# Gate sums moved from GpSimd to VectorE, and a layer's small loads issued one by one along its projection

## What is computed

```python
h = rms_norm(x, norm1_g[l])
parts = jnp.split(h @ w_in[l], cuts, axis=-1)        # w_in: 1024 x 2144, q/k/v of four token mixers
o_a, o_b, o_c, o_d = four attention mixers, 256 wide each
...
br = jnp.stack([o_a, o_b, o_c, o_d], axis=2)
y = jnp.einsum('bsnc,ncd->bsnd', br, w_branch[l])    # four branches, 256 -> 1024
g = jax.nn.sigmoid(h @ w_gate[l] + b_gate[l]).reshape(B, S, N_BRANCH, D)
x = x + jnp.sum(g * y, axis=2) @ w_o[l]              # the gated sum over branches
h2 = rms_norm(x, norm2_g[l])
x = x + jnp.square(jax.nn.relu(h2 @ w_ff1[l])) @ w_ff2[l]
```

## Time and profile before

| | us |
|---|---|
| median of 3 runs (lowest to highest) | 840.53 (839.75 to 841.16) |
| the profiled execution, its own time | 840.49 |
| its span in the trace | 838.7 |
| TensorE products busy | 818.3 (98%) |
| VectorE busy | 540.9 (64%) |
| ScalarE busy | 411.1 (49%) |
| GpSimd busy | 83.6 (10%) |

### The profile page before, as it was taken

One profiled execution on the slowest core, in us unless ns is written; L12 is line 12 of the kernel. 1 busy time (PEld: TensorE's weight loads), 2 busy tenths in 40 slices (PEclk: granted clock), 3 DMA queues, 4 the chain that ended last, 5 costly groups with the idle time before them and its releaser, 6 DMA issues.

```text
span 838.7 us, 14823 instructions
## 1 busy us (share of the span) xinstructions
PE 818.3 (98%) x5763; PEld 750.5 (89%) x5763; DVE 540.9 (64%) x781; ACT 411.1 (49%) x698; POOL 83.6 (10%) x105
## 2 busy tenths in 40 slices
PE   7699999999999999999999999999999999999996
PEld 7699988999889999999999999799997999999995
DVE  6486566957667555666568756578756675555663
ACT  6346565655365333444464466466444553334442
POOL 3220000202310000000033000002221100000000
PEclk9899999999999999999999999999999999999999
DMA  8956633454437555555576755344344565565541
GB/s 254 246 167 209 172 108 101 121 182 150 127 100 229 199 200 196 184 167 184 178 194 201 220 151 153 127 123 128 109 167 129 192 218 190 200 200 190 171 141 50
DMA packets 100850, 141.09 MB, mean 168 GB/s; under 512 B 4796, under 2 KB 87040, under 8 KB 100800
## 3 DMA queue, kind: packets, MB, share of 16 engines
q1 hardware_dynamic: 99296, 137.12, 51.5%
q0 software_dynamic: 1216, 3.17, 1.5%
q10 hardware_dynamic: 288, 0.11, 0.1%
HBM read 139.33 MB, written 1.05 MB: 167 GB/s over the span
## 4 chain that ended last, share of the span: by engine, by line
PE 78%; issue 12%; DVE 4%; POOL 3%; DMA 2%; ACT 1%; POOLq 0%; ACTq 0%; DVEq 0%
PE bank_w L1185 16%; PE bank_w L1187 16%; PE bank_w L1186 16%; PE bank_acc L1185 8%; PE bank_acc L1186 8%; PE bank_acc L1187 8%; POOL mix L543 2%; DMA raw<-in_w_in 2%; DVE w_lo L808 2%; PE bank_acc L1281 2%; PE bank_acc L1293 1%; PE bank_o L1310 1%; DVE act_lo L1003 1%; DVE tmp L1023 1%; DMA cst<-in_table 0%
## 5 line engine op out<-in xcount | busy, mean ns | idle before, releaser
L808 DVE TENSOR_TENSOR w_lo<-raw,w_hi 128x1024 fp32r<-128x1024 f32 (+1 forms) x256 | 309.9, 1257 | 58.4 <-ACT w_hi L573 58.2
L1185 PE MATMUL bank_w<-act_hi,w_hi 128*128 128x256 f32 x1008 | 287.9, 286 | 0.0
L1187 PE MATMUL bank_w<-act_hi,w_lo 128*128 128x256 f32 x1008 | 285.8, 284 | 0.0
L1186 PE MATMUL bank_w<-act_lo,w_hi 128*128 128x256 f32 x1008 | 285.3, 283 | 0.0
L573 ACT ACTIVATE w_hi<-raw 128x1024 fp32r<-128x1024 f32 (+1 forms) x256 | 257.4, 1060 | 37.6 <-DMA raw<-in_w_in 19.8
L1185 PEld LDWEIGHTS bank_w<-act_hi,w_hi 128*128 128x128 f32 x1008 | 191.6, 190 | 7.1 <-ACT big L694 3.1
L1186 PEld LDWEIGHTS bank_w<-act_lo,w_hi 128*128 128x128 f32 x1008 | 190.9, 189 | 1.8 <-issue 0.5
L1187 PEld LDWEIGHTS bank_w<-act_hi,w_lo 128*128 128x128 f32 x1008 | 191.2, 190 | 0.0
L702 ACT ACTIVATE part_hi<-big 128x512 fp32r<-128x512 f32 x32 | 20.2, 633 | 189.8 <-DVE big L1038 187.1
L1185 PE MATMUL bank_acc<-w_hi,part_hi 128*128 128x512 f32 x256 | 100.3, 392 | 0.0
L1186 PE MATMUL bank_acc<-w_lo,part_hi 128*128 128x512 f32 x256 | 100.3, 392 | 0.0
(11 more groups left out here) (180 smaller groups left out, 983.6 us busy)
## 6 DMA issues: line engine op xcount, KB each, us to landing
raw<-in_w_ff SPq DMA_DIRECT2D x128, 512.0 KB, 4.9
raw<-in_w_gate SPq DMA_DIRECT2D x64, 512.0 KB, 4.7
raw<-in_w_in SPq DMA_DIRECT2D x32, 536.0 KB, 5.3
raw<-in_w_o SPq DMA_DIRECT2D x16, 512.0 KB, 4.8
raw<-in_w_branch SPq DMA_DIRECT2D x16, 256.0 KB, 4.6
raw<-in_w_branch SPq DMA_DIRECT2D x8, 512.0 KB, 4.2
xs<-in_x SPq DMA_DIRECT2D x2, 512.0 KB, 4.1
out_y<-big SPq DMA_DIRECT2D x4, 256.0 KB, 2.1
```

The lines of the kernel that those rows point to most:

```text
L808: nc.vector.tensor_tensor(half_view(w_lo, c, hf), raw_half(c, hf), f32(half_view(w_hi, c, hf)), ALU.subtract).then_inc(w_lo_ready, 1)
L1185: nc.tensor.matmul(dst, s_hi, m_hi, start=first, stop=False)
L1186: nc.tensor.matmul(dst, s_hi, m_lo, start=False, stop=False)
L1187: ins = nc.tensor.matmul(dst, s_lo, m_hi, start=False, stop=last)
```

## The change

GpSimd's 12 adds a layer (L543) are gone. VectorE makes each of them itself right behind its product (after a wait for that product's own semaphore), and no longer waits for `mixed` before it writes `tmp`. The last branch (`y` 3) is taken out of the step loop: its four quarters are written out with the `w_lo` halves of `o` 2 and the four `mix_lo` in between. The small loads of a layer are issued in groups, each of which waits until ScalarE has rounded the second half of a given chunk of the projection: the table `cst` (first layer only), both gains and the sink behind chunk 3; one half of the bias rows behind chunk 4; the other half behind chunk 5 and behind the inverse roots for mixer A; `w_uq` behind 6; `w_ukv` behind 7. `hi_count(l, c, h)` is the count of `w_hi_ready` at which half h of chunk c is rounded.

```diff
             for l in range(DEPTH):
                 norm(2 * l, l)
+                pool.wait_ge(w_hi_ready, hi_count(l, 3, 1))
                 if l == 0:
-                    pool.wait_ge(w_hi_ready, 5)
                     pool.dma_start(cst[:, C_ID + P:], table[:, C_ID + P:]).then_inc(cst_landed, 16)
-                for r in range(2):
-                    (bias row r: the same DMA as bias_run(l, r))
                 pool.dma_start(gain_qk[:, 0, :], ...)
                 pool.dma_start(gain_qk[:, 1, :], ...)
                 pool.dma_start(sink[:, :], ...)
-                pool.dma_start(w_uq[:, 0, :], ...)
-                pool.dma_start(w_uq[0:QR - P, 1, :], ...)
-                pool.dma_start(w_ukv[:, :], ...)
-                pool.wait_ge(sink_landed, l * 16 + 16)
-                nc.gpsimd.tensor_tensor(nsink[:, :], sink[:, :], neg_one[:, :], ALU.mult).then_inc(nsink_ready, 1)
+                pool.wait_ge(w_hi_ready, hi_count(l, 4, 1))
+                bias_run(l, 0)
                 pool.wait_ge(ss_a_ready, l + 1)
                 inverse_root(rs_a, ss_a, inv_head, l).then_inc(rs_a_ready, 1)
+                pool.wait_ge(w_hi_ready, hi_count(l, 5, 1))
+                bias_run(l, 1)
+                pool.wait_ge(sink_landed, l * 16 + 16)
+                nc.gpsimd.tensor_tensor(nsink[:, :], sink[:, :], neg_one[:, :], ALU.mult).then_inc(nsink_ready, 1)
+                pool.wait_ge(w_hi_ready, hi_count(l, 6, 1))
+                pool.dma_start(w_uq[:, 0, :], ...)
+                pool.dma_start(w_uq[0:QR - P, 1, :], ...)
+                pool.wait_ge(w_hi_ready, hi_count(l, 7, 1))
+                pool.dma_start(w_ukv[:, :], ...)
...
-                for k in range(4 * (NB - 1)):
-                    pool.wait_ge(y_read, l * 16 + (k + 5))
-                    if k >= 4:
-                        pool.wait_ge(mixed, l * 12 + (k - 3))
-                    nc.gpsimd.tensor_tensor(mix[:, k % 4, :], mix[:, k % 4, :], tmp[:, k % 2, :], ALU.add).then_inc(mixed, 1)
-                pool.wait_ge(mixed, l * 12 + 12)
                 norm(2 * l + 1, l)
...
                     k = 4 * (n - 1) + q
-                    if k >= 2:
-                        dve.wait_ge(mixed, l * 12 + (k - 1))
                     nc.vector.scalar_tensor_tensor(out=tmp[:, k % 2, :], in0=g, scalar=1.0, in1=y, op0=ALU.add,
                                                    op1=ALU.mult).then_inc(y_read, 1)
-                    if n == NB - 1 and 0 < q < 3:
-                        mix_lo(q - 1, l)
+                    dve.wait_ge(y_read, l * 16 + (k + 5))
+                    nc.vector.tensor_tensor(mix[:, q, :], mix[:, q, :], tmp[:, k % 2, :], ALU.add).then_inc(mixed, 1)
...
+                branch(NB - 1, l, (0,))
                 split_lo_half(POS["o", 2], 0, l)
+                branch(NB - 1, l, (1,))
+                mix_lo(0, l)
+                split_lo_half(POS["o", 2], 1, l)
+                branch(NB - 1, l, (2,))
+                mix_lo(1, l)
+                branch(NB - 1, l, (3,))
                 mix_lo(2, l)
-                split_lo_half(POS["o", 2], 1, l)
                 mix_lo(3, l)
                 split_lo(POS["o", 3], l)
```

More of the change, by code:

```diff
@@ L498, in norm, with bias_run @@
                     nc.gpsimd.tensor_tensor(rstd[:, t:t + 1], total, neg_half[:, 0:1], ALU.pow).then_inc(rstd_ready, 1)
+            def bias_run(l, r):
+                at = (NA_ROWS - 4 + r) * BIAS_ROW + NA_COLS - GRID_W
+                tables = b_rel_bias[bass.ds(l, 1), 0]
+                src = bass.AP(tensor=tables.tensor, offset=tables.offset + at,
+                              ap=[[1, GRID_W], [(2 * NA_ROWS - 1) * BIAS_ROW, H], [1, RUN]])
+                pool.dma_start(run[r * GRID_W:(r + 1) * GRID_W, :, :], src).then_inc(bias_landed, 16)
             for l in range(DEPTH):
                 norm(2 * l, l)
+                uq = d_w_uq[bass.ds(l, 1)].rearrange("o k n -> (o k) n")
+                pool.wait_ge(w_hi_ready, hi_count(l, 3, 1))
                 if l == 0:
-                    pool.wait_ge(w_hi_ready, 5)
                     pool.dma_start(cst[:, C_ID + P:], table[:, C_ID + P:]).then_inc(cst_landed, 16)
-                for r in range(2):
-                    at = (NA_ROWS - 4 + r) * BIAS_ROW + NA_COLS - GRID_W
-                    tables = b_rel_bias[bass.ds(l, 1), 0]
-                    src = bass.AP(tensor=tables.tensor, offset=tables.offset + at,
-                                  ap=[[1, GRID_W], [(2 * NA_ROWS - 1) * BIAS_ROW, H], [1, RUN]])
-                    pool.dma_start(run[r * GRID_W:(r + 1) * GRID_W, :, :], src).then_inc(bias_landed, 16)
                 pool.dma_start(gain_qk[:, 0, :], a_q_norm_g[bass.ds(l, 1), :].to_broadcast([P, HD])).then_inc(gains_landed, 16)
@@ L513, in _ @@
                 pool.dma_start(sink[:, :], c_sink[bass.ds(l, 1), :].to_broadcast([P, H])).then_inc(sink_landed, 16)
-                uq = d_w_uq[bass.ds(l, 1)].rearrange("o k n -> (o k) n")
-                pool.dma_start(w_uq[:, 0, :], uq[0:P, :]).then_inc(lat_landed, 16)
-                pool.dma_start(w_uq[0:QR - P, 1, :], uq[P:QR, :]).then_inc(lat_landed, 16)
-                pool.dma_start(w_ukv[:, :], d_w_ukv[bass.ds(l, 1)].rearrange("o k n -> (o k) n")).then_inc(lat_landed, 16)
-                pool.wait_ge(sink_landed, l * 16 + 16)
-                nc.gpsimd.tensor_tensor(nsink[:, :], sink[:, :], neg_one[:, :], ALU.mult).then_inc(nsink_ready, 1)
+                pool.wait_ge(w_hi_ready, hi_count(l, 4, 1))
+                bias_run(l, 0)
                 pool.wait_ge(ss_a_ready, l + 1)
@@ L523, in _ @@
                              inv_head[:, :], l).then_inc(rs_a_ready, 1)
+                pool.wait_ge(w_hi_ready, hi_count(l, 5, 1))
[3 more added lines that the diff above has]
+                pool.wait_ge(w_hi_ready, hi_count(l, 6, 1))
+                pool.dma_start(w_uq[:, 0, :], uq[0:P, :]).then_inc(lat_landed, 16)
+                pool.dma_start(w_uq[0:QR - P, 1, :], uq[P:QR, :]).then_inc(lat_landed, 16)
+                pool.wait_ge(w_hi_ready, hi_count(l, 7, 1))
+                pool.dma_start(w_ukv[:, :], d_w_ukv[bass.ds(l, 1)].rearrange("o k n -> (o k) n")).then_inc(lat_landed, 16)
                 pool.wait_ge(cst_landed, 16)
@@ L1073, in _ @@
                         heads_lo(i, l)
-                    if kind == "y":
+                    if kind == "y" and j < NB - 1:
                         branch(j, l, (0, 1))
@@ L1090, in _ @@
                         normalise(i, l)
-                    if kind == "y":
+                    if kind == "y" and j < NB - 1:
                         branch(j, l, (2, 3))
-                        if j < NB - 1:
-                            for c in SPLIT_AT[s]:
-                                split_lo(c, l)
+                        for c in SPLIT_AT[s]:
+                            split_lo(c, l)
                     if s == 8:
```

## The result

| | before | after |
|---|---|---|
| median, us | 840.51 (839.75 to 841.16, 4 runs) | 835.95 (835.62 to 837.63, 4 runs) |
| ratio, 95% interval | | 0.9944 (0.9932 to 0.9957) |
| the profiled execution, us | 840.49 | 837.63 |
| TensorE / VectorE / GpSimd busy, us | 818.3 / 540.9 / 83.6 | 817.3 / 544.5 / 42.8 |

What follows compares the result with a forecast made beforehand. TensorE, busy 98% of the span, was taken to bound the kernel, gaining only where it stands or runs slowly: 840.49 - 6.76 - 1.75 + 0.7 - 0.4 = 832.28, forecast 832.3 us, range 830.3 to 838 (0.85).

Steps and rivals of the forecast that it cites:

- its own case: Whole kernel: the forecast of 832.3 us with ends 830.3 and 835.2, chance 0.70.
- `a_norm`: First projection: GpSimd's inverse roots ready at 35.6 us, just in time for VectorE; cost 0, bounds -0.5 and +1.0 us.
- rival 1: At `a_norm`, inverse roots come late and VectorE, then TensorE, stands: 1 to 3 us a layer, 834 to 838; chance 0.15.
- the large gain: First projection, ahead of and in chunk 3: 6.76 us of TensorE standing and 1.75 us of lowered clock both go.
- What is late next: First projection: chunk 5 lands late, `in_evac(3)` behind it, TensorE stands ahead of chunk 4 for 0.7 us (0 to 2.0).
- the price of the burst: First small loads, 0.78 MB, half of all, delay the load of chunk 5's second half by 3.2 to 5.2 us.
- So short a stand should leave the clock where it is: First projection, ahead of chunk 4: a 0.7 us stand leaves the granted clock at its upper level, no cost.
- the bias adds are later too, with the same answer: GpSimd's bias adds, 3.81 us, are first wanted beside the seventh gate chunk, far behind; cost nothing.
- The cost of nothing for the second layer: Second layer's projection: TensorE never stands there before the change, so the loads win nothing and cost nothing.
- The sums: Adds moved to VectorE: branches 1 and 2 cost nothing, last branch and `w_o` gain 0.2 us a layer, 0.4 in all.
- Rival 3: All three branches: VectorE's 24 adds fully exposed, 16.4 us, giving 848.4 us; chance 0.05.
- Rival 2: The burst hits chunk 5 as it hit chunk 4: 6.7 us stand plus 1.75 us of clock, 840.0 us; chance 0.08.

Runs made afterwards that it cites:

- after_again: The changed kernel unaltered, measured again beside other kernels: 837.99 us against 840.66 for the kernel before, ratio 0.9969; its trace 835.75 us.
- spread: bias_adds_late with table, bias halves, `w_uq` and `w_ukv` each behind its own later chunk, gains and sink still behind chunk 3: 831.98 us, ratio 0.9896.
- bias_adds_late: The changed kernel, with GpSimd's four bias adds of mixer B waiting until VectorE has copied the projection's last chunk: 836.15 us, ratio 0.995.
- loads_late: loads_only with GpSimd's bias adds waiting until VectorE has copied the projection's last chunk: 835.47 us, ratio 0.993.
- loads_only: The kernel before with only the changed kernel's order of small loads, sums still on GpSimd: 839.23 us, ratio 0.997.
- port_probe: spread plus three unused GpSimd additions of 128x384 a layer beside VectorE's rotation of mixer A: 832.7 us, ratio 0.9906.
- spread_gpsimd_sums: spread with the 12 adds a layer back on GpSimd: 832.32 us, ratio 0.9901.
- late_no_gains: bias_adds_late without the loads of both gains and the sink (ones instead): 831.94 us, ratio 0.9894.

## Why the prediction was right where it was, and wrong where it was

**The number: inside the range by luck.** The forecast was 832.3 and its own case ended at 835.2; 835.95 lies above. The range went on to 838 for a late `a_norm` (rival 1), and that did not happen. after_again's trace, 835.75 us, shows what filled the gap to the forecast: a stand longer than the term by 2.0 us (2.68 against 0.7), the bias adds in the first layer 1.05, a start later by 0.36, and 0.2 that can't be placed, 3.6 in all, where 3.5 were missing. The changed kernel's first trace has 0.5 us more of the stand and 1.45 more for the bias adds in the second layer.

**Place and mechanism of the large gain: right.** The stand of 6.76 us and the clock behind it were the small loads' doing, chunks 3 and 4 now land in time, and with everything out of the way 8.0 of the 8.51 us came back in the projection (spread).

**What is late next: right name, wrong size.** Chunk 5's second half, `in_evac(3)` behind it, a stand ahead of chunk 4, were named as they came. The term was 0.7 us with ends 0 and 2.0; it was 3.18, and 2.68 in the second trace. The load was issued at 26.8 us and took 10.6 instead of 7.4 to 9.4, so it lies above the upper end as well. The mis-sized term is the price of the burst, "half of the 1.57" MB and so 3.2 to 5.2 us. By the kernels that leave parts of it out it was 6.3, of which gains and sink, counted as 66 KB, are 3.3. With 6.3 the same working gives 26.8 + 3.7 + 0.5 + 6.3 = 37.3, and the load landed at 37.3. A part of the 6.3 may be the weight loads' own: those issued at 18 to 21 us, ahead of any small load, took 5.2 to 5.5 us, and not 3.7 + 0.5. The halving itself was sound for the place it was taken from: in the kernel before, table, gains, sink and half the bias rows took 3.3 of the queue's 6.4 us. What failed is carrying this price over, since the same burst took 5.0 us of the engines in its new place. The table was also issued only 2.0 us ahead of the load (24.8 and 26.8), where "three us" was the reason for the lower end.

**"So short a stand should leave the clock where it is": wrong as a certainty.** The clock stayed up in both traces of the changed kernel (stands of 3.18 and 2.68 us), and fell in those of bias_adds_late (2.69), loads_late (3.08) and loads_only (3.29), in each 0.8 to 1.5 us after the stand, for 3.41 us. This costs 1.5 us, and the length of the stand doesn't decide it here; the range should have held it as a term of its own.

**"the bias adds are later too, with the same answer": the step that failed outright.** It asked only by when their result is wanted. The text itself had said, for `a_norm` and for the sums, that GpSimd's adds stretch VectorE; moving them off `a_norm` was booked as a help, and where they would land instead was not looked up. They landed beside mixer A's rotation and the `w_lo` behind it: 1.0 us in the first layer, 1.45 or nothing in the second. Their fixed place in the order (behind the wait for chunk 7) was in the diff. The Trainium skill's rule on the shared port pair ("SBUF — State Buffer", section "SBUF: two separate sides"), cited in the prediction for the sums, was the right one; what it does here is in port_probe's 3.63 against 1.16 us. The cost of nothing for the second layer fell with it.

**`a_norm`: right.** The inverse roots were ready at 33.9 us, ahead of VectorE at 40.1, and its six multiplications take 1.29 instead of 3.84 us. Rival 1 did not happen, and not only because the stand made VectorE late: in spread, without a stand, the roots were ready at 33.9 and VectorE came at 36.9, and in the changed kernel's second layer at 446.4 and 447.7.

**The sums: right.** Forecast 0.4 us of gain for both layers; the leads show 0.23 in each layer of the changed kernel, and spread against spread_gpsimd_sums 0.2. Branch 1 after, where two adds and the `prob` steps lie side by side:

```profile
154.38 0.69 DVE L1026 TENSOR_TENSOR mix<-mix,tmp 128x512 f32<-128x512 f32 x1
...
156.71 0.62 DVE L987 TENSOR_SCALAR prob<-prob,rsum 128x256 f32<-128x256 f32 x2
...
158.16 0.68 DVE L1023 SCALAR_TENSOR_TENSOR tmp<-big,bank_w 128x512 f32<-128x512 f32 x1
...
160.81 2.35 DVE L810 TENSOR_TENSOR w_lo<-raw,w_hi 128x1024 fp32r<-128x1024 f32 x2
```

The third read starts at 158.16, which is 161.94 on the clock of the kernel before (lead 3.78), where it started at 162.05; the `w_lo` pair is through in 2.35 us. In the last branch TensorE stood 0.46 us before its fourth quarter (forecast 0.6; by the starts of the products the lead falls by 0.6 to 0.7), by TensorE's timeline:

```profile
214.36 0.39 PE L1190 MATMUL bank_w<-part_hi,w_hi 128*128 128x256 f32 x1 [0.46 <-DVE tmp L1023]
```

The lead across the branch and `w_o` went from 3.88 to 4.01, so 0.13 us where 0.2 was forecast; another 0.10 a layer comes from a product ahead of that branch (at 193.95 us before), which was forecast at nothing. Rival 3 did not happen. Rival 2, the stand that moves by a chunk, did in part: 3.18 of its 6.7 us, and, in the kernels with the same burst, in some executions the clock as well. It had 0.08 and was set against the forecast as all or nothing, where the truth lay between the two.

## What to carry to other kernels

Measure what a burst of small loads costs the load behind it in its new place, part by part; neither its bytes nor its price in the old place tells it. Here 66 KB of short rows, each a copy of one row, cost that load 3.3 us, as much as 0.7 MB of table and bias rows; the stand went when either of the two was taken out of the load's way. When a step moves on one engine, ask not only by when its result is wanted but what it will run beside in its new place, above all on engines that share a port, and let it wait for an event there rather than for a load. A short stand can cost the clock as well, in some executions and not in others, so a kernel whose runs scatter by 4 us may hide an edit worth 2: measure it in a variant where the other stands are gone.

## What the runs showed of the hardware

- Gains and sink, 384 rows and 66 KB, took 2.6 us of all 16 DMA engines in spread; table and half the bias rows, 0.7 MB, took 2.5 in late_no_gains. In the kernel before, gains and sink took 0.8.
- The granted clock fell to its lower level 0.8 to 1.5 us after stands of 2.69, 3.08 and 3.29 us (bias_adds_late, loads_late, loads_only), stayed there for 3.41 us, and did not fall after stands of 3.18 and 2.68 (the changed kernel's two traces).
- GpSimd's four additions held one VectorE addition with two SBUF inputs from 0.96 to 4.42 us, nearly their whole run of 3.61 (changed kernel, second layer). When they started 0.45 us later (after_again), they alternated with `w_lo` halves: two of these took 4.00 us instead of 2.46, and three of the additions 4.81.
